# Feed-forward loop: three of eight gate and up tile pairs as 2x2 blocks in seven products

## What is computed

```python
D_FF = -(-(8 * D_MODEL) // (3 * 256)) * 256
...
        ff = (jax.nn.silu(h2 @ w_ffn_gate[l]) * (h2 @ w_ffn_up[l])) @ w_ffn_down[l]
        x = x + g2 * ff
    return rms_norm(x, final_w)
```

## Time and profile before

| | us |
|---|---|
| median of 3 runs | 2235.67 |
| lowest and highest | 2235.11, 2240.11 |
| the profiled execution's own time | 2236.0 |
| its span | 2234.3 |
| a turn of the loop in it | 65.3 |

### The profile page before, as it was taken

The page is one execution under the profiler, slowest core; times in us unless marked ns, Lnnn a source line. Parts: engine busy times, 40 slices in busy tenths (PEclk is TensorE's granted clock), DMA queues, the critical chain, the costliest instruction groups (busy, mean ns, idle before and its releaser), DMA issues.

```text
span 2234.3 us, 31225 instructions
## 1 busy us (share of the span) xinstructions
PE 2220.6 (99%) x10287; PEld 1849.4 (83%) x10287; DVE 1623.7 (73%) x2120; ACT 1103.8 (49%) x1437; POOL 136.8 (6%) x259
## 2 busy tenths in 40 slices
PE   9999999999999999999999999999999999999998
PEld 8888888888888888888888888888888888888886
DVE  6767777878875876888788777766665666666576
ACT  6555446666664445433466554444444443344444
POOL 1100110000000000010011110000000000000000
PEclk9999999999999999999999999999999999999999
DMA  8878896656665765697589987666766776766664
GB/s 321 326 246 308 309 338 234 219 196 210 219 218 193 287 230 195 234 332 268 191 303 324 303 293 253 242 210 213 235 222 231 238 241 228 238 232 223 211 218 147
DMA packets 157899, 551.78 MB, mean 247 GB/s; under 512 B 19441, under 2 KB 25328, under 8 KB 156288
## 3 DMA queue, kind: packets, MB, share of 16 engines
q1 hardware_dynamic: 112416, 405.92, 52.7%
q0 software_dynamic: 34304, 129.64, 16.7%
q10 hardware_dynamic: 11104, 15.22, 2.0%
HBM read 534.92 MB, written 10.53 MB: 244 GB/s over the span
## 4 chain that ended last, share of the span: by engine, by line
PE 96%; DVE 2%; DMA 1%; ACT 1%; issue 0%; SPq 0%; DVEq 0%; ACTq 0%
PE ps L2091 23%; PE ps L2092 23%; PE ps L2093 23%; PE ps L2209 6%; PE ps L2211 6%; PE ps L2210 6%; PE ps L2130 2%; PE ps L2339 1%; DMA raw<-ws_dram 1%; PE ps L2106 1%; PE ps L2108 1%; PE ps L2107 1%; DMA late<-wa_dram 1%; DVE w_lo L1197 0%; PE ps L2269 0%; PE ps L2533 0%
## 5 line engine op out<-in xcount | busy, mean ns | idle before, releaser
L1197 DVE TENSOR_TENSOR w_lo<-raw,w_hi 128x1024 fp32r<-128x1024 f32 x757 | 921.0, 1223 | 513.3 <-ACT w_hi L675 499.2
L675 ACT ACTIVATE w_hi<-raw 128x1024 fp32r<-128x1024 f32 x749 | 788.5, 1060 | 970.9 <-PE ps L2093 820.4
L2091 PE MATMUL ps<-w_hi,a_hi 128*128 128x512 f32 x1612 | 629.3, 390 | 0.1
L2093 PE MATMUL ps<-w_hi,a_lo 128*128 128x512 f32 x1612 | 627.5, 389 | 0.0
L2092 PE MATMUL ps<-w_lo,a_hi 128*128 128x512 f32 x1612 | 627.3, 389 | 0.0
L2093 PEld LDWEIGHTS ps<-w_hi,a_lo 128*128 128x128 f32 x1612 | 302.6, 188 | 63.3
L2091 PEld LDWEIGHTS ps<-w_hi,a_hi 128*128 128x128 f32 x1612 | 302.7, 188 | 62.8 <-DVE w_lo L1197 0.3
L2092 PEld LDWEIGHTS ps<-w_lo,a_hi 128*128 128x128 f32 x1612 | 302.7, 188 | 61.8
L2209 PE MATMUL ps<-w_hi,a_hi 128*128 128x512 f32 x640 | 256.0, 400 | 1.9 <-ACT gst L769 1.9
L2211 PE MATMUL ps<-w_hi,a_lo 128*128 128x512 f32 x640 | 250.3, 391 | 0.0
L2210 PE MATMUL ps<-w_lo,a_hi 128*128 128x512 f32 x640 | 250.0, 391 | 0.0
(11 more groups left out here) (366 smaller groups left out, 2263.3 us busy)
## 6 DMA issues: line engine op xcount, KB each, us to landing
raw<-ws_dram SPq DMA_DIRECT2D x768, 512.0 KB, 4.3
ada<-wa_dram POOLq DMA_DIRECT2D x140, 512.0 KB, 4.8
late<-wa_dram POOLq DMA_DIRECT2D x35, 512.0 KB, 5.4
late_c<-wa_dram POOLq DMA_DIRECT2D x17, 512.0 KB, 5.2
gates_spill<-gst ACTq DMA_DIRECT2D x16, 512.0 KB, 5.6
...
```

Source lines behind the costliest of these rows:

```text
L675: act.activation(w_hi[:, k.slot(RING), :], raw[:, k.slot(RING), :], ACT.Copy).then_inc(hi_done, 1)
L1197: dve.tensor_tensor(w_lo[:, k.slot(RING), :], raw[:, k.slot(RING), :], w_hi[:, k.slot(RING), :].bitcast(F32), ALU.subtract).then_inc(lo_do ...
L2091: pe.matmul(o, hi(m, tb), w_hi[:, s, cols], start=m == 0, stop=False)
L2093: mm = pe.matmul(o, lo(m, tb), w_hi[:, s, cols], start=False, stop=m == of * kts - 1)
```

## The change

In the loop a *quad* is one gate and one up tile of the same features: a 2 x 2 product, tokens (two blocks) by features (two blocks) times features by columns (gate, up). Tiles are reordered so that gate and up tiles alternate. Quads 2, 4 and 6 of a turn's eight (tiles 4 and 5, 8 and 9, 12 and 13) are made with seven block products in place of eight (`mixed_quad`); the other five as before. That takes

- four sums of activation blocks per quad (`mix_s`, made once before the loop, `act_mix`), with their two parts `mix_s_hi` and `mix_s_lo`;
- four sums of weight blocks per quad and turn, 512 columns each, by VectorE from the raw tiles (`mixed_sums`, `mix_w`), rounded by ScalarE (`mixed_hi`, `mix_hi`) and subtracted by VectorE (`mixed_lo`, `mix_lo`, 2048 columns). There is one buffer of each: a quad's rounding waits until TensorE is done with the quad before. Of the up tile only the second half is still split itself;
- three more accumulators in banks 4 to 7, which VectorE joins with the gate and up sums at the turn's end (`g_part`, `u_part`); the down products move to banks 4 to 7 as well.

Besides, the 16 transfers of f move from ScalarE to GpSimd (`send_f`), behind the turn's modulation loads there; f is turned at the end of its own turn; the modulations move to four other places of the turn; `final_b` is loaded later. The core of the diff:

```diff
+QUADS = (2, 4, 6)
+MIXED_END = 2 * QUADS[-1] + 2
...
-            with pool.Fori(1, KT) as i:
-                for k in range(2):
-                    pool.wait_ge(ada2_used, 2 * i + (k - 1))
-                    pool.dma_start(ada3[:, k, :], wa[2 * i + (ADA0["ff"] + k)]).then_inc(ada2_landed[k], 16)
...
+            def send_f(sent):
+                pool.wait_ge(f_lanes, sent)
+                pool.sem_inc(f_asked, 1)
+                for b in range(4):
+                    for i in range(4):
+                        pool.dma_start(turned[32 * b:32 * b + 32, i], lanes[32 * i:32 * i + 32, b]).then_inc(f_turned, 16)
...
+            def load_ada2(m):
+                pool.wait_ge(ada2_used, (m + -1).n)
+                pool.dma_start(ada3[:, m.slot(2), :], wa[(m + ADA0["ff"]).n]).then_inc(ada2_landed[m.slot(2)], 16)
+
+            send_f(1)
+            with pool.Fori(1, turns_ff) as j:
+                for m in range(n):
+                    load_ada2(At(2 - n + m, n, j))
+                send_f(At(1, 1, j).n)
+            for m in range(2):
+                load_ada2(At(n * turns_ff - 2 + m))
+            send_f(turns_ff + 1)
+            send_f(FC - 1)
...
-            def steps_sending_f(k, j):
-
-                act.wait_ge(f_lanes, (j + 1).n)
-                z, turned = (x[:].rearrange("p a t k s -> p a (t k s)") for x in (fz, fT))
-                for b in range(4):
-                    for i in range(4):
-                        act.dma_start(turned[32 * b:32 * b + 32, i], z[32 * i:32 * i + 32, b]).then_inc(f_turned, 16)
-                    steps(k + b, 1)
-
...
+            def mixed_hi(j, n, freed):
+
+                sums0 = At(4 * len(QUADS) * (j.base - 1) + 4 * n, 4 * len(QUADS) * j.per, j.i)
+                act.wait_ge(tile_used, freed.n)
+                act.wait_ge(w_mix_sum, (sums0 + 2).n)
+                act.activation(mix_hi[:, 0:2], mix_w[:, 0:2], ACT.Copy)
+                act.wait_ge(w_mix_sum, (sums0 + 4).n)
+                act.activation(mix_hi[:, 2:4], mix_w[:, 2:4], ACT.Copy)
...
+                def step(p):
+                    at_ = p + RING
+                    if at_ // 2 not in QUADS:
+                        split(k + at_)
+                    elif at_ % 2:
+                        n = QUADS.index(at_ // 2)
+                        mixed_hi(j, n, k + (2 * QUADS[n - 1] + 2 - (0 if n else per)))
+                        split_half(k + at_)
+                    else:
+                        split(k + at_)
+
...
+                for p in range(4):
+                    step(p)
+                act_hi(j + -1)
+                for p in range(4, 2 * T_K - 1):
+                    step(p)
+                    if p + 1 == MIXED_END:
+                        act.wait_ge(tile_used, (k + MIXED_END).n)
+                        act.activation(g_part[:, 0], ps[:, 4, :], ACT.Copy).then_inc(first_copied, 1)
+                act.wait_ge(act_ready, j.n)
+                act.wait_ge(gate_up_free, At(2 * j.base + 1, 2 * j.per, j.i).n)
+                act.activation(f_silu[:], g_part[:, 0:3:2], ACT.Silu).then_inc(silu_done, 1)
+                for p in range(2 * T_K - 1, per):
+                    step(p)
...
+            def act_mix():
+
+                dve.wait_ge(t_free, TG["norm3"] + 8 + 2)
+                for n, q in enumerate(QUADS):
+                    hi, lo = (x[:, 2 * q:2 * q + 2, :].bitcast(F32).rearrange("p k (t s) -> p k t s", t=TB) for x in (a_hi, a_lo))
+                    chain.on(dve.tensor_tensor(mix_x[:, n], hi, lo, ALU.add))
+                dve.wait_ge(dve_chain, chain.n)
+                chain.on(dve.tensor_tensor(mix_s[:, :, 0], mix_x[:, :, 0, 1], mix_x[:, :, 1, 1], ALU.add))
+                link(dve.tensor_tensor(mix_s[:, :, 2], mix_x[:, :, 0, 0], mix_x[:, :, 0, 1], ALU.subtract))
+                link(dve.tensor_tensor(mix_s[:, :, 1], mix_s[:, :, 0], mix_x[:, :, 0, 0], ALU.subtract))
+                link(dve.tensor_tensor(mix_s[:, :, 3], mix_x[:, :, 1, 0], mix_s[:, :, 1], ALU.subtract))
+                dve.sem_inc(act_mixed, 1)
+
...
+            def mixed_sums(k, j, n):
+
+                g, u = raw[:, k.slot(RING)], raw[:, (k + 1).slot(RING)]
+                sums0 = At(4 * len(QUADS) * (j.base - 1) + 4 * n, 4 * len(QUADS) * j.per, j.i)
+                for x in (k, k + 1):
+                    dve.wait_ge(raw_landed[x.slot(RING)], x.lap(RING, 16))
+                dve.tensor_tensor(mix_w[:, 0], u[:, 0:NC], g[:, 0:NC], ALU.subtract).then_inc(w_mix_sum, 1)
+                dve.tensor_tensor(mix_w[:, 1], u[:, NC:TW], u[:, 0:NC], ALU.subtract).then_inc(w_mix_sum, 1)
+                dve.wait_ge(w_mix_sum, (sums0 + 1).n)
+                dve.tensor_tensor(mix_w[:, 2], u[:, NC:TW], mix_w[:, 0], ALU.subtract).then_inc(w_mix_sum, 1)
+                dve.wait_ge(w_mix_sum, (sums0 + 3).n)
+                dve.tensor_tensor(mix_w[:, 3], g[:, NC:TW], mix_w[:, 2], ALU.subtract).then_inc(w_mix_sum, 1)
...
+            def mixed_lo(k):
+
+                slot = k.slot(RING)
+                dve.wait_ge(hi_done, (k + 1).n)
+                dve.tensor_tensor(mix_lo[:], mix_w[:], mix_hi[:].bitcast(F32), ALU.subtract)
+                dve.tensor_tensor(w_lo[:, slot, NC:TW], raw[:, slot, NC:TW], w_hi[:, slot, NC:TW].bitcast(F32), ALU.subtract)\
+                    .then_inc(lo_done, 1)
...
+                sums(0)
+                step(0)
+                step(1)
+                step(2)
+                modulated(0)
+                step(3)
                 act_lo(j + -1)
+                sums(1)
+                step(4)
+                step(5)
+                step(6)
+                step(7)
+                sums(2)
+                step(8)
+                modulated(1)
+                step(9)
+                step(10)
+                step(11)
+                step(12)
+                modulated(2)
+                dve.wait_ge(first_copied, j.n)
+                part0 = At(2 * j.base - 2, 2 * j.per, j.i)
+                dve.tensor_tensor(g_part[:, 1], ps[:, 6, :], g_part[:, 0], ALU.add).then_inc(part_sum, 1)
+                dve.wait_ge(part_sum, (part0 + 1).n)
+                dve.tensor_tensor(g_part[:, 2], ps[:, 7, :], g_part[:, 1], ALU.add).then_inc(part_sum, 1)
+                dve.wait_ge(part_sum, (part0 + 2).n)
+                dve.tensor_tensor(u_part[:], ps[:, 5, :].unsqueeze(1).to_broadcast([P, TB, NC]), g_part[:, 1:3], ALU.add)\
+                    .then_inc(parts_free, 1)
+                step(13)
+                dve.wait_ge(parts_free, j.n)
+                dve.wait_ge(tile_used, (k + (2 * T_K - 1)).n)
+                dve.tensor_tensor(g_part[:, 0:3:2], gate_bank, g_part[:, 0:3:2], ALU.add).then_inc(gate_up_free, 1)
+                step(14)
+                dve.wait_ge(tile_used, (k + 2 * T_K).n)
+                dve.tensor_tensor(u_part[:], up_bank, u_part[:], ALU.add).then_inc(gate_up_free, 1)
+                dve.wait_ge(silu_done, j.n)
+                dve.wait_ge(gate_up_free, At(2 * j.base + 2, 2 * j.per, j.i).n)
+                dve.tensor_tensor(f_act[:], u_part[:], f_silu[:], ALU.mult).then_inc(act_ready, 1)
+                step(15)
+                dve.wait_ge(act_ready, (j + 1).n)
+                turn_lanes()
+                dve.wait_ge(down_free, At(4 * j.base, 4 * j.per, j.i).n)
+                for c in range(4):
+                    step(2 * T_K + 2 * c)
+                    b = 4 + 2 * (c % 2)
+                    dve.wait_ge(tile_used, (k + (2 * T_K + (c + 1) * T_Q)).n)
+                    dve.tensor_tensor(acc[:, c], ps[:, b:b + 2, :], acc[:, c], ALU.add).then_inc(down_free, 1)
+                    step(2 * T_K + 2 * c + 1)
+                    if c == 1:
+                        modulated(3)
...
+                q = QUADS[n]
+                g, u = k.slot(RING), (k + 1).slot(RING)
+                first, last = n == 0, n == len(QUADS) - 1
...
+                def product(out, hi, lo, whi, wlo, opens=False, closes=False):
+                    pe.matmul(out, hi, whi, start=opens, stop=False)
+                    pe.matmul(out, hi, wlo, start=False, stop=False)
+                    return pe.matmul(out, lo, whi, start=False, stop=closes)
+
+                def mixed(out, s, w, **group):
+                    return product(out, mix_s_hi[:, n, s], mix_s_lo[n][:, s], mix_hi[:, w], mix_lo[:, w], **group)
+
+                pe.wait_ge(lo_done, (k + 1).n)
+                product(ps[:, 4, :], ah(2 * q, 0), al(2 * q, 0), w_hi[:, g, 0:NC], w_lo[:, g, 0:NC], first, last)
+                product(gate_bank[:, 0], ah(2 * q + 1, 0), al(2 * q + 1, 0), w_hi[:, g, NC:TW], w_lo[:, g, NC:TW])\
+                    .then_inc(tile_used, 1)
+                pe.wait_ge(lo_done, (k + 2).n)
+                product(up_bank[:, 0], mix_s_hi[:, n, 3], mix_s_lo[n][:, 3], w_hi[:, u, NC:TW], w_lo[:, u, NC:TW])
+                product(gate_bank[:, 1], ah(2 * q + 1, 1), al(2 * q + 1, 1), mix_hi[:, 3], mix_lo[:, 3])
```

(54 more changed lines are left out.)

125 lines of the change are left out of this document (67 added, 58 removed).

## The result

The changed kernel takes 2246.95 us in the median (2239.96 to 2250.83, 8 runs), the kernel before in the same series 2234.43 (2232.58 to 2240.11, 8 runs): ratio 1.0051, 95% interval 1.0036 to 1.0065. It is slower by about 12 us, where 8 less were forecast. The profiled execution took 2249.22 us.

A forecast was written before the change was run, and what follows sets the result against it. TensorE was taken as the bound, busy 99%. Savings of 8.7 (seven turns) + 2.0 (ninth) - 0.3 (first) = 10.4 us, less 2.4 for pick-ups, gave 8.0 off 2236.0: 2228.0 us; range 2222 to 2239, the forecast's own 2222 to 2231.

The forecast's parts named there:

- the transfers of f: Moved from ScalarE to GpSimd behind the fourth modulation load; from turn 2 landed by 69.2 us, needed at 76.1, 6.9 spare.
- timetable: Predicted start and end times in one turn, zero at TensorE's start on tile 0; a turn takes 64.04 us.
- free at 3.17: VectorE, done with the turn before and the loop's end, can start the first sums 3.17 us into the turn.
- lost at the third quad: TensorE stalls 0.8 us per turn on a chain of load, sums, tile, modulation and low halves.
- pick-ups: Starts behind a wait, set at 0.04 us; about four on the path, 0.1 more each, 2.4 us in seven turns.
- Removed matmuls: Three quads in nine turns drop 81 matmuls at 0.2267 us, 18.4 us; a turn would be 63.24, 2.04 less.
- The raw load of tile 13: Load that the third sums need, taken to land 3.2 us after issue; 4.15 is the bad end.
- rival 1: Raw loads stay at 4.15 us, third-quad stall 1.75, a turn 65.0: 2234.3 us, no change; chance 15%.
- The down tiles: ScalarE copies bank 4 by 38.6, VectorE joins products by 41.3, TensorE wants the banks at 42.3: no stall.
- The first turn: ScalarE waits 2.6 us for f, delaying the second quad; eats that turn's gain and about 0.3 us more.
- rival 2: VectorE's 30 short instructions take about 0.09 us more each; stall 2.3, a turn 65.55: 2238 us; chance 12%.
- Rival 3: Small transfers issue slowly on GpSimd, deciding from 0.96 us each; at 1.2, f is 3.8 late: 2254 us; chance 8%.

## Why the prediction was wrong, step by step

**The step that failed** is the one on the transfers of f: "covered with 6.9 us to spare". It asked only when f itself would arrive. In that it was right (GpSimd issues 0.49 us apart, 0.53 taken; ScalarE waits for f once, 1.2 us in the first turn, where 2.6 was counted), though less was to spare: in the third turn f has landed by 1692.9 at the latest, and ScalarE takes it at 1695.51, 2.6 us later. It did not ask what 512 KB more, directly behind a 512 KB modulation load, do to the raw loads of the same 13 us, and one of those is what the first sums wait for. With it failed the timetable's first line, "free at 3.17", which took tiles 4 and 5 as landed. The prediction bounded a raw load's price at 4.15 us; here it was 9.1, the first sums started 3.5 us too late, and with f ahead of the fourth load, where it was 5.6, they started on time. The trace of before has f by itself. Its transfers in the third turn,

```profile
L1118 ACTq DMA_DIRECT2D fT<-fz x16: 514/612/685, 1689.4 to 1699.1; - x16
```

begin 4.7 us after the issue of the last modulation load (1684.73), and modulation loads land there in 3.9 to 4.9 us. Raw loads issued ahead of f took 4.3 to 4.8 us, those beside it 3.5 to 3.9.

**The timetable from there on was right.** With f moved out of the crowd, the third turn runs on it, from TensorE's start on the turn at 1676.90:

| | timetable | measured |
|---|---|---|
| first sums start | 3.17 | 3.23 |
| first half tile done | 10.26 | 10.40 |
| second half tile done | 22.08 | 22.09 |
| third sums start | 25.5 | 25.70 |
| third half tile done | 33.33 | 33.41 |
| lost at the third quad | 0.8 | 0.82 |

One sum in it is 0.1 too long: the third sums, started at 25.5, would end at 28.05 by the 2.55 that they were given, not at 28.15; they took 2.54. A turn is then 64.62 us, 64.04 forecast and 64.38 with the pick-ups. That this kernel's 2227.0 comes within 1 us of the 2228.0 forecast for the change is in part luck: the kernel before ran at 2233.57 beside it, so the gain is 6.5 us, not 8.0.

**Removed matmuls:** 81, 0.227 each, right; the ninth turn is 63.3. **VectorE's load:** 58.0 us a turn, 58.5 counted. **The raw load of tile 13:** 3.2 was chosen; 3.1 was measured in the changed kernel, so rival 1 is out. **The down tiles:** "no stall" was wrong by 0.2 us a turn; VectorE waits there for the copy behind a rounding that waits for its load. **The first turn** lost about 3 us (0.5, 0.9 and 1.4 at its second and third quad and its down tiles) where 2.3 was counted.

**Rivals.** Gaps at all three quads were to mean rival 2, the full duration of VectorE's short instructions. They came without it: 1689.48 to 1690.09 is 0.61 start to start for an instruction of 0.69. The Trainium skill (VectorE: DVE Perf Modes, The DRAIN you can't avoid) says first that the next instruction waits for the empty pipe, and then, in the same paragraph, that one which is not held starts earlier; the prediction took up only the first. At 512 columns, too, this trace shows the early start. Rival 3 had the right place, f on GpSimd, with the wrong mechanism (the pace of issue) and so the wrong test. No case had a transfer that is on time itself and makes others late.
